# First products of the next stage between the last turns of two norms, projection weights by way of the raw buffer, and attention inputs turned a unit later

## The chip, the core and the metric

The kernel runs on one core of a Trainium2 chip. The metric is the device time of one execution in microseconds. The core has TensorE (PE in the profile; PEld is its weight load), VectorE (DVE), ScalarE (ACT), GpSimd (POOL) and SyncE (SP), each with a queue of its own, and 16 DMA engines. They meet only at semaphores.

## The reference

Two transformer layers on 1024 tokens of width 1024, all in float32. The parts that matter here, in the order in which the program comes to them:

```
h = rmsnorm(x, g_mix); z = h @ w_in                       # first layer
q_na, k_na = rmsnorm(...) per head; q = rmsnorm(q_mem); k, v = mem_n @ w_mem_kv
gates = sigmoid(gate_pre)                                  # 3 x 1024 columns of z
y = gates0 * (h_m @ w_proj_mlstm) + gates1 * (h_na @ w_proj_na) + gates2 * (h_mem @ w_proj_mem)
x = x + y @ w_out
u = rmsnorm(x, g_ffn) @ w_up                               # 4096 columns
x = x + square(relu(u)) @ w_down
h = rms_norm(x, attn_norm); proj = h @ w_in_2              # second layer: delta net, retention, experts
```

## The kernel before

The program is a chain of stages. Each stage is a block: every engine runs its own list for the stage, written out in the code, and all of them start the next block together. Within a block the order on an engine is fixed by the code, and an engine waits at a semaphore for what it needs. PSUM has eight banks of 128 x 512 numbers, `c.bank(i)`.

A float32 matrix product is made of three: each operand is split in an upper part (a rounded copy) and a lower part (the rest), and `PASSES` runs upper x upper, upper x lower and lower x upper. So a product over eight k tiles is 24 matmuls of 512 columns, and one over four k tiles is 12. Weights arrive in chunks of 1 MB: SP loads a chunk in the one raw buffer, `c.raw` (`load_chunks`, issued at L102); VectorE splits it in one of two places of `c.split_ring` (`split_chunk`), which takes a wait for the chunk two places back to be used up (`c.used`); TensorE waits for the split (`wait_split`). The next load waits for that split.

**Attention inputs** (`attention_inputs`). There are 18 units: 8 for q and k of the neighbourhood attention, 8 for its v and the memory's q, 2 for the memory's k and v. A unit is one block of 128 tokens; its product has two halves, r = 0 and r = 1, of 12 matmuls each with a weight chunk each. Units go in runs of four: the first halves of the run, then the second halves. After a unit's second half ScalarE copies and squares it, VectorE sums the squares, GpSimd takes the power -0.5, VectorE scales the rows (L1172), and TensorE turns them (L1071) in one of two banks, from which VectorE copies them (L1144) when it is at the unit two further on. TensorE keeps the finished units in the list `waiting`; a turn is put into its queue after a half product by rules on the length of that list. `NEXT_SPLIT` says before which unit VectorE splits the next weight chunk.

**Gated branches** (`gated_branches`). The gates are made first by `SevenProducts`: two blocks of columns as quarters in the ordinary way, and the other ten (W = 10) as seven half-size products each, for which VectorE and ScalarE make operands and sums. Results go out over tiles to DRAM (`gate_rows`). In the last of the ten blocks the steps turn over to the projections: SP loads the first two pieces of projection weights (v = 0, 1), VectorE splits them (`split_pw`), ScalarE takes the upper parts of the branches' outputs (`take_acts`), VectorE the lower ones (`lower_act`). Then TensorE does the 48 projections, which wait for `pw_split`, `acts_split` and the evictions, and VectorE multiplies each with the gates read back from DRAM.

**Norms at a stage's end** (`project_norm` and the end of `ffn`). The last product of a stage adds a residual, and each block of 128 tokens is normalised, turned by TensorE in two groups of four transposes (`TileNorm.turn`, L431, banks 0 to 3), copied as the upper part by ScalarE (L439) and as the lower part by VectorE (L138). The turn of a block follows the products by three blocks (`LAG`), so turns 5, 6 and 7 stand behind all products. Two of the three such norms are touched: the one before the feed-forward stage (`out1`) and the one at its end (`ff`).

**What comes behind them.** The feed-forward stage begins with `SevenProducts` again (eight quarters of 24 matmuls, then W = 14 blocks of seven products of 12), and the second layer with `delta_inputs`, 24 products of 24 matmuls for a convolution.

## Time and profile before

| | |
|---|---|
| three timed runs | 3031.94, 3036.04, 3036.41 us; median 3036.04 |
| the profiled execution's own time | 3034.09 us |
| its span, first to last instruction | 3032.3 us |
| granted TensorE clock, mean | 0.959 of full speed |
| TensorE busy | 2770.4 us, 91% |
| VectorE busy | 1456.2 us, 48% |
| ScalarE, GpSimd busy | 780.2 us, 345.8 us |

The stages of the change lie at these times of the span: attention inputs from 261 to 383 us, gates and projections from 515 to 850, the norm of `out1` up to 956, the feed-forward stage to 1635, `delta_inputs` to 1837. The experts of the second layer load their weights in the last 600 us, at around 400 GB/s.

In a timeline row stand the start, the time taken, the engine, the line of the kernel, the operation, what it writes and reads, its shape and how many instructions the row merges; in brackets the idle time of the engine before it and what ended that. "PEq" and "SPq" as a releaser or an engine are the queue of the engine. TensorE's matmuls are pipelined: one starts while the one before is in flight, so starts are compared, not ends.

### The profile page before, as it was taken

Reading aid. Unit: us, or ns where it says so; the run is one execution under the profiler, and the core shown is the slowest. Engines: PE = TensorE matmul, PEld = TensorE weight load, DVE = VectorE, ACT = ScalarE, POOL = GpSimd, SP = SyncE. Lnnn points to the kernel's source line nnn. Section 1 sums busy time; section 2 is a strip of 40 time slices with the busy share of each in tenths; the row PEclk is TensorE's granted clock in tenths of the full one; section 3 lists DMA queues with packets and bytes.
Section 4 is the critical chain, followed back from the end, with each engine's and each line's share of the span. In section 5 each row is a group of like instructions: output and inputs, shape, how many; then the busy total and the mean of one; then the engine's idle time right before and its main releaser. Section 6 shows DMA issues by size and latency. Waiting matters only on the chain. (4 is left out here: it accounts for less than half of the span.)

```text
span 3032.3 us, 43019 instructions
## 1 busy us (share of the span) xinstructions
PE 2770.4 (91%) x17136; PEld 2156.1 (71%) x17136; DVE 1456.2 (48%) x2428; ACT 780.2 (26%) x1729; POOL 345.8 (11%) x497
## 2 busy tenths in 40 slices
PE   7998988999999999999999998899999878888886
PEld 5876755887777888878887896777887745545443
DVE  6656487765756666543355643554434431111113
ACT  3244176433013555300003423330021201111111
POOL 1023300000001000000001003540020211111112
PEclk9998999999999999999999998999999979999998
DMA  4130121233632334432234220002102199999995
GB/s 149 43 91 18 56 93 34 93 112 118 198 122 97 102 111 139 170 108 94 84 97 99 46 39 2 2 2 70 42 18 109 66 385 417 415 414 406 404 399 210
DMA packets 162152, 430.08 MB, mean 142 GB/s; under 512 B 18585, under 2 KB 64793, under 8 KB 144545
## 3 DMA queue, kind: packets, MB, share of 16 engines
q1 hardware_dynamic: 146128, 392.04, 36.4%
q10 hardware_dynamic: 5312, 18.48, 1.7%
q0 software_dynamic: 10512, 16.80, 1.5%
q8 instruction: 137, 2.24, 0.3%
q14 instruction: 63, 0.51, 0.0%
HBM read 382.76 MB, written 65.08 MB: 148 GB/s over the span
## 5 line engine op out<-in xcount | busy, mean ns | idle before, releaser
L489 PE MATMUL banks<-split_weights,hT_upper 128*128 128x512 f32 x1536 | 482.9, 396 | 14.3 <-DVE hT_lower L138 8.6
L489 PEld LDWEIGHTS banks<-split_weights,hT_upper 128*128 128x128 f32 x1536 | 290.8, 191 | 76.9 <-issue 14.5
L489 PE MATMUL banks<-split_weights,uT_upper 128*128 128x512 f32 x1024 | 317.2, 391 | 2.7 <-DVE uT_lower L138 2.6
L489 PE MATMUL banks<-split_weights,hT_lower 128*128 128x512 f32 x768 | 303.0, 395 | 0.0
L3529 PE MATMUL banks<-expert_inner,ex_xT 128*64 128x256 f32 (+1 forms) x1248 | 217.6, 400 | 34.4 <-DVE ex_xT L3629 10.7
L498 PE MATMUL banks<-hT_upper,split_weights 128*128 128x512 f32 x736 | 234.0, 396 | 9.2 <-DVE split_weights L138 4.4
L3640 DVE COPY ex_y<-banks 128x512 f32<-128x512 f32 x36 | 24.9, 691 | 434.8 <-PE banks L3558 434.8
L489 PEld LDWEIGHTS banks<-split_weights,uT_upper 128*128 128x128 f32 x1024 | 192.6, 189 | 43.5 <-issue 3.5
L489 PE MATMUL banks<-split_weights,uT_lower 128*128 128x512 f32 x512 | 200.2, 391 | 0.0
L3529 PEld LDWEIGHTS banks<-expert_inner,ex_xT 128*64 128x64 f32 (+1 forms) x1248 | 139.6, 150 | 79.1 <-issue 47.6
L1901 PE MATMUL banks<-hT_upper,split_weights 128*128 128x512 f32 x576 | 189.1, 389 | 0.0
L138 DVE TENSOR_TENSOR split_weights<-raw_weights,split_weights 128x512 fp32r<-128x512 f32 (+1 forms) x128 | 177.7, 1388 | 5.0 <-ACT split_weights L1921 3.0
L489 PEld LDWEIGHTS banks<-split_weights,hT_lower 128*128 128x128 f32 x768 | 146.2, 190 | 31.3
L498 PEld LDWEIGHTS banks<-hT_upper,split_weights 128*128 128x128 f32 x736 | 140.4, 191 | 39.3 <-issue 5.4
L498 PE MATMUL banks<-hT_lower,split_weights 128*128 128x512 f32 x368 | 145.0, 394 | 0.0
L134 DVE CAST split_weights<-raw_weights 128x2048 fp32r<-128x2048 f32 x56 | 68.4, 1221 | 132.9 <-PE banks L489 42.8
L1901 PEld LDWEIGHTS banks<-hT_upper,split_weights 128*128 128x128 f32 x576 | 108.2, 188 | 22.3
L2207 DVE TENSOR_TENSOR x<-x,banks 128x512 f32<-128x512 f32 x64 | 43.9, 685 | 165.2 <-PE banks L489 165.2
L1901 PE MATMUL banks<-br_sums,split_weights 128*128 128x512 f32 x480 | 113.7, 389 | 0.0
L3558 PE MATMUL banks<-expert_inner,ex_hT 128*64 128x512 f32 (+1 forms) x312 | 106.3, 618 | 7.2 <-issue 6.4
L3529 PE MATMUL banks<-hT,ex_xT 128*64 128x256 f32 (+1 forms) x416 | 101.0, 399 | 12.5 <-DMA expert_inner<-in_w_up 5.9
L1901 PE MATMUL banks<-hT_lower,split_weights 128*128 128x512 f32 x288 | 112.1, 389 | 0.0
(554 smaller groups left out, 5074.0 us busy)
## 6 DMA issues: line engine op xcount, KB each, us to landing
expert_inner<-in_w_gate SPq DMA_DIRECT2D x39, 1024.0 KB, 13.1
expert_inner<-in_w_up SPq DMA_DIRECT2D x39, 1024.0 KB, 22.5
expert_inner<-in_w_down SPq DMA_DIRECT2D x38, 1024.0 KB, 24.5
raw_weights<-in_w_in SPq DMA_DIRECT2D x28, 1024.0 KB, 6.5
uT_whole<-u_rows ACTq DMA_DIRECT2D x32, 512.0 KB, 5.6
raw_weights<-in_w_down SPq DMA_DIRECT2D x16, 1024.0 KB, 5.1
raw_weights<-in_w_up SPq DMA_DIRECT2D x28, 512.0 KB, 4.1
hT<-in_w_gate SPq DMA_DIRECT2D x13, 1024.0 KB, 12.0
```

The source lines that it names most:

```text
L134: return engine.tensor_copy(dst.bitcast(F32R), src)
L138: return engine.tensor_tensor(dst.bitcast(F32R), whole, upper, ALU.subtract)
L489: last = pe.matmul(bank, acts[x][:, r * KT // 2 + k, m * P:(m + 1) * P].bitcast(F32R), w[y][:, k, :].bitcast(F32R), start=(r == 0 and k == ...
L498: last = pe.matmul(out, w[x][:, k, c0:c0 + P].bitcast(F32R), acts[y][:, k, t0:t0 + nt].bitcast(F32R), start=(k == 0 and x == y), stop=(k = ...
L1901: last = pe.matmul(self.bank(w, i), x_parts[x][:, k, :].bitcast(F32R), y_parts[y][:, k, :].bitcast(F32R), start=(k == 0 and x == y), stop= ...
L2207: nc.vector.tensor_tensor(x, x, c.bank(m), ALU.add).then_inc(added, 1)
L3529: last = nc.tensor.matmul(c.psum[cols, BANKS[q], i * D_EXPERT:(i + 1) * D_EXPERT], xT[:, q, k, cols], w[:, k, :], start=(k == 0), stop=(k ...
L3558: last = nc.tensor.matmul(c.psum[cols, 4 + b, :], hT[:, f, cols], experts.down[s][:, f, b * BANK:(b + 1) * BANK], start=(f == 0), stop=(f ...
L3640: nc.vector.tensor_copy(y[:, q, BANK:D], c.bank(5)).then_inc(y_dve, 1)
```

## The change

**Attention inputs.** The turn of a unit comes one half product later: while second halves run, a turn is put in only when more than four units wait (before: more than three), or when the run is the last one. The splits of the next chunks come before units 4, 8, 12 and 14 (before: 5, 8, 13 and 16). At the end both marks that the last two chunks are used are set together by ScalarE.

**Gated branches.** The first two pieces of projection weights are loaded in the raw buffer, when all operands of the last block are made, in place of another buffer when its third product is done. VectorE splits the first piece after the third step of the last block (before: after the fourth), and the lower parts of the first branch follow one step sooner as well. The load of the first chunk of `w_out` waits for both splits, since it overwrites the raw buffer.

**The two norms.** Behind turn 5, turn 6 and turn 7 stand eight matmuls each of the next stage's first product, in bank 4. They wait for that bank's last addition, the lower parts of the first four blocks of tokens, and the weights. The next stage leaves its first product out, and its banks are rotated by four, so that the rest follows on.

```diff
+def next_products(pe, c, hT, j, out):
+    w = c.parts(j)
+    for k in range(KT):
+        for x, y in PASSES:
+            yield pe.matmul(out, w[x][:, k, 0:P].bitcast(F32R), hT[y][:, k, 0:BANK].bitcast(F32R),
+                            start=(k == 0 and x == y), stop=(k == KT - 1 and x == 1))
+AHEAD_BANK = 4
...
-    NEXT_SPLIT = {5: C_NAV, 8: C_NAV + 1, 13: C_MEMKV, 16: C_MEMKV + 1}
+    NEXT_SPLIT = {4: C_NAV, 8: C_NAV + 1, 12: C_MEMKV, 14: C_MEMKV + 1}
...
-                            if len(waiting) > 3:
+                            if len(waiting) > RUN or run[-1] + 1 == n:
                                 turn(waiting.pop(0))
                             continue
-                        if i + 1 == n or (i == run[-1] and units[i + 1][0] != j):
+                        if i + 1 < n and i == run[-1] and units[i + 1][0] != j:
                             last.then_inc(c.used, 1)
...
-                if i + 1 == n or units[i + 1][0] != j:
+                if i + 1 == n:
+                    act.sem_inc(c.used, 2)
+                elif units[i + 1][0] != j:
                     act.sem_inc(c.used, 1)
...
+        raw = c.raw[:, :, :].rearrange("p k n -> p (k n)")
+        def pw_whole(v):
+            if v < 2:
+                return raw[:, v * D:(v + 1) * D].rearrange("p (a b n) -> p a b n", a=2, b=2)
+            return pw(h_plain[1], v)
...
                 else:
-                    sp.wait_ge(gates.product, 7 * (W - 1) + 3)
+                    sp.wait_ge(gates.made, 7 * W)
...
             def after_first(w):
                 if w == W - 1:
-                    for v in range(2):
-                        load_pw(v)
+                    sp.wait_ge(gates.product, 7 * w + 3)
                     gates.wait_stored(sp, 5)
...
-            gates.transfers(sp, after_first, None)
+            def after_block(w):
+                if w == W - 2:
+                    for v in range(2):
+                        load_pw(v)
+            gates.transfers(sp, after_first, after_block)
             gates.wait_stored(sp, 3 * N)
-            sp.wait_ge(gates.made, 7 * W)
+            sp.wait_ge(pw_split, 2)
             c.load_chunks(sp, C_OUT + 1)
...
-                if i == 3:
+                if i == 2:
                     split_pw(0)
-                if i in (4, 5):
-                    lower_act(0, 2 * (i - 4))
-                    lower_act(0, 2 * (i - 4) + 1)
+                if i in (3, 4):
+                    lower_act(0, 2 * (i - 3))
+                    lower_act(0, 2 * (i - 3) + 1)
...
+            soon = None if ahead is None else next_products(nc.tensor, c, acts, ahead, c.bank(AHEAD_BANK))
             for i in range(TT - LAG, TT):
                 norm.turn(pe, i)
                 route(i - 2)
+                if soon is not None:
+                    if i == TT - LAG:
+                        pe.wait_ge(added, TT + AHEAD_BANK + 1)
+                        pe.wait_ge(norm.copied, TT)
+                        c.wait_split(pe, ahead)
+                    for _ in itertools.islice(soon, KT):
+                        pass
...
     def bank(self, w, i):
-        return self.c.bank((7 * w + i) % 8)
+        return self.c.bank((7 * w + i + self.first_bank) % 8)
...
+            if i == 0 and self.first_done:
+                continue
+            last = split_channels(pe, self.quarter_bank(i), self.hT, (i % 2) * BANK, BANK, c.parts(j), (i // 2 % 2) * P)
+            last.then_inc(self.quarter, 2 if i == 1 and self.first_done else 1)
...
                             if f + n + h == 0:
-                                if m < 2:
-                                    pe.wait_ge(up.evicted, 7 * W - 1 + m)
+                                up.wait_bank(pe, m)
...
+            soon = next_products(nc.tensor, c, hT, C_IN2, c.bank(AHEAD_BANK))
             for i in range(TT - LAG, TT):
                 norm.turn(pe, i)
+                if i == TT - LAG:
+                    pe.wait_ge(added, LAST + AHEAD_BANK + 1)
+                    pe.wait_ge(norm.copied, TT)
+                    c.wait_split(pe, C_IN2)
+                for _ in itertools.islice(soon, KT):
+                    pass
...
                     if g >= NB:
                         pe.wait_ge(copied, g - NB + 1)
-                    split_channels(nc.tensor, c.bank(g % NB), hT, th * BANK, BANK, c.parts(C_IN2 + ch // 2), ch % 2 * P).then_inc(product, 1)
+                    if g:
+                        last = split_channels(nc.tensor, c.bank(AHEAD_BANK + g % NB), hT, th * BANK, BANK, c.parts(C_IN2 + ch // 2), ch % 2 * P)
+                        last.then_inc(product, 2 if g == 1 else 1)
```

TensorE's order at the end of the first norm, before: the last products of the stage (L489), the turns (L431, the last four as one row of 32 transposes), then the next stage's first product (L498).

```order
L489 MATMUL banks<-split_weights,hT_upper 128x512 x2
L489 MATMUL banks<-split_weights,hT_lower 128x512
L431 MATMUL banks<-c_ident,out_xn 128x128 x32
L1589 UNCONDITIONAL_BRANCH
L2105 UNCONDITIONAL_BRANCH
L498 MATMUL banks<-hT_upper,split_weights 128x512
L498 MATMUL banks<-hT_lower,split_weights 128x512
L498 MATMUL banks<-hT_upper,split_weights 128x512 x2
```

The same place now (L443 is the turn, L378 `next_products`): turns 4 and 5 in one row, eight matmuls, turn 6, and the beginning of the next eight.

```order
L443 MATMUL banks<-c_ident,out_xn 128x128 x16
L378 MATMUL banks<-hT_upper,split_weights 128x512
L378 MATMUL banks<-hT_lower,split_weights 128x512
L378 MATMUL banks<-hT_upper,split_weights 128x512 x2
L378 MATMUL banks<-hT_lower,split_weights 128x512
L378 MATMUL banks<-hT_upper,split_weights 128x512 x2
L378 MATMUL banks<-hT_lower,split_weights 128x512
L443 MATMUL banks<-c_ident,out_xn 128x128 x8
L378 MATMUL banks<-hT_upper,split_weights 128x512 x2
L378 MATMUL banks<-hT_lower,split_weights 128x512
```

The 24 matmuls of the next stage's first product moved in front of the two block ends, in three groups of eight behind the last three turns. The end of the `ff` norm reads likewise.

TensorE's order at the start of the last run of the attention inputs, before: the last product half of unit 15 (from hT), the turn of unit 12 (L1071), then the first half of unit 16 (from at_mem).

```order
L489 MATMUL banks<-split_weights,hT_upper 128x512 x2
L489 MATMUL banks<-split_weights,hT_lower 128x512
L1071 MATMUL banks<-c_ident,at_raw 128x128 x2
L489 MATMUL banks<-split_weights,at_mem_upper 128x512 x2
L489 MATMUL banks<-split_weights,at_mem_lower 128x512
```

The same place now (L1083 is the turn, L501 the products):

```order
L501 MATMUL banks<-split_weights,hT_upper 128x512 x2
L501 MATMUL banks<-split_weights,hT_lower 128x512
L501 MATMUL banks<-split_weights,at_mem_upper 128x512 x2
L501 MATMUL banks<-split_weights,at_mem_lower 128x512
L501 MATMUL banks<-split_weights,at_mem_upper 128x512 x2
L501 MATMUL banks<-split_weights,at_mem_lower 128x512
L501 MATMUL banks<-split_weights,at_mem_upper 128x512 x2
L501 MATMUL banks<-split_weights,at_mem_lower 128x512
L501 MATMUL banks<-split_weights,at_mem_upper 128x512 x2
L501 MATMUL banks<-split_weights,at_mem_lower 128x512
L1083 MATMUL banks<-c_ident,at_raw 128x128 x2
```

The turn of unit 12 moved behind unit 16's first half. In the same way each turn of the earlier runs stands one half product later.

VectorE's order in the last of the ten gate blocks, before: evictions of half-size products (L1970), the split of the first piece of projection weights (hT_upper, hT_lower from hT), the lower parts of the branches (branches_lower), the second split.

```order
L1970 TENSOR_TENSOR br_gate_pair<-hT_spare,banks 128x512
L1970 TENSOR_TENSOR hT<-hT_spare,banks 128x512
L134 CAST hT_upper<-hT 128x2x512
L138 TENSOR_TENSOR hT_lower<-hT,hT_upper 128x2x512
L1970 TENSOR_TENSOR br_gate_pair<-hT,banks 128x512
L1970 TENSOR_TENSOR hT_spare<-hT_spare,banks 128x512
L138 TENSOR_TENSOR branches_lower<-x,br_sums 128x1024 x2
L1970 TENSOR_TENSOR hT_spare<-hT,banks 128x512
L138 TENSOR_TENSOR branches_lower<-x,br_sums 128x1024 x2
L1970 TENSOR_TENSOR hT_spare<-hT_spare,banks 128x512
L134 CAST hT_upper<-hT 128x2x512
```

The same place now (L2020 is the eviction):

```order
L2020 TENSOR_TENSOR br_gate_pair<-hT_spare,banks 128x512
L134 CAST hT_upper<-raw_weights 128x2x512
L138 TENSOR_TENSOR hT_lower<-raw_weights,hT_upper 128x2x512
L2020 TENSOR_TENSOR hT<-hT_spare,banks 128x512
L138 TENSOR_TENSOR branches_lower<-x,br_sums 128x1024 x2
L2020 TENSOR_TENSOR br_gate_pair<-hT,banks 128x512
L2020 TENSOR_TENSOR hT_spare<-hT_spare,banks 128x512
L138 TENSOR_TENSOR branches_lower<-x,br_sums 128x1024 x2
L2020 TENSOR_TENSOR hT_spare<-hT,banks 128x512
L2020 TENSOR_TENSOR hT_spare<-hT_spare,banks 128x512
L134 CAST hT_upper<-raw_weights 128x2x512
```

The first split, now from the raw buffer, and the four lower parts moved up by one eviction each; the second split kept its place.

## Rows read from the trace of the kernel before

**Rows 1.** Section 1 of the page: busy us, share of the span, instructions.

```profile
PE 2770.4 (91%) x17136; PEld 2156.1 (71%) x17136; DVE 1456.2 (48%) x2428; ACT 780.2 (26%) x1729; POOL 345.8 (11%) x497
```

**Rows 2.** Busy us by stretch, down projection: PE, PEld, DVE, ACT, POOL, PEclk, DMA.

```profile
1268.00:1620.00 352.00, 349.42 (x1546) 289.12 (x1547) 155.78 (x160) 11.86 (x22) 5.31 (x11) 1.00 0.34 117
```

**Rows 3.** Timelines by engine, last gate block and first projection.

```profile
732.93 0.69 DVE L138 TENSOR_TENSOR split_weights<-raw_weights,split_weights 128x512 fp32r<-128x512 f32 x1
...
742.24 0.98 SPq L1463 DMA_DIRECT2D hT<-in_w_proj_mlstm  x2
...
743.21 3.90 ACT L1521 ACTIVATE br_sums<-x 128x1024 fp32r<-128x1024 f32 x4 [1.36 <-PE banks L1901]
...
746.99 0.69 DVE L134 CAST hT_upper<-hT 128x1024 fp32r<-128x1024 f32 x1 [3.09 <-DMA hT<-in_w_proj_mlstm]
...
752.92 2.35 DVE L138 TENSOR_TENSOR branches_lower<-x,br_sums 128x1024 fp32r<-128x1024 f32 x2
...
755.37 0.76 PE L1513 MATMUL banks<-br_sums,hT_upper 128*128 128x512 f32 x1 [4.04 <-issue]
...
761.35 0.40 PE L1513 MATMUL banks<-br_sums,hT_lower 128*128 128x512 f32 x1
```

**Rows 4.** Timelines by engine, attention inputs.

```profile
285.35 0.60 PE L1071 MATMUL banks<-c_ident,at_raw 128*128 128x128 f32 x4
...
296.56 0.76 DVE L1172 SCALAR_TENSOR_TENSOR at_raw<-at_raw,at_rstd 128x256 f32<-128x256 f32 x2 [2.70 <-POOL at_rstd L1134]
...
297.37 0.66 PE L1071 MATMUL banks<-c_ident,at_raw 128*128 128x128 f32 x4 [1.24 <-DVE at_raw L1172]
...
304.66 0.69 DVE L1162 TENSOR_REDUCE at_ss<-at_squares 128x16 f32<-128x512 f32 x1 [7.34 <-ACT at_squares L1125]
...
326.76 1.22 DVE L134 CAST split_weights<-raw_weights 128x2048 fp32r<-128x2048 f32 x1
...
333.42 0.38 ACT L1118 ACTIVATE at_raw<-banks 128x256 f32<-128x256 f32 x1 [20.27 <-PE banks L489]
...
369.35 1.22 DVE L134 CAST split_weights<-raw_weights 128x2048 fp32r<-128x2048 f32 x1
...
372.95 0.74 PE L489 MATMUL banks<-split_weights,at_mem_upper 128*128 128x512 f32 x2 [2.37 <-DVE split_weights L138]
...
382.12 0.58 PE L1071 MATMUL banks<-c_ident,at_raw 128*128 128x128 f32 x2 [2.39 <-DVE at_raw L1172]
```

**Rows 5.** Timelines by engine, first norm's end and the next stage.

```profile
947.58 1.16 PE L431 MATMUL banks<-c_ident,out_xn 128*128 128x128 f32 x8 [0.71 <-DVE hT_lower L138]
...
952.36 1.94 PE L431 MATMUL banks<-c_ident,out_xn 128*128 128x128 f32 x8 [1.23 <-DVE hT_lower L138]
...
954.97 0.69 DVE L138 TENSOR_TENSOR hT_lower<-banks,hT_upper 128x512 fp32r<-128x512 f32 x1 [0.16 <-ACT hT_upper L439]
...
955.98 0.77 PE L498 MATMUL banks<-hT_upper,split_weights 128*128 128x512 f32 x1 [1.68 <-PEq L1589]
...
963.21 0.60 ACT L1909 ACTIVATE ff_relu<-banks 128x512 f32<-128x512 f32 x1 [8.27 <-PE banks L498]
```

**Rows 6.** Busy time by stretch, at the ends of both norms.

```profile
950.00:955.00 5.00, 3.08 (x16) 2.35 (x16) 4.73 (x8) 2.38 (x5) 0.00 (x0) 0.73 0.00 0
...
1630.00:1635.00 5.00, 1.16 (x8) 0.84 (x8) 3.66 (x7) 1.35 (x3) 0.00 (x0) 1.00 0.00 0
```

**Rows 7.** Timelines by engine, second norm's end and the next stage.

```profile
1630.82 1.16 PE L431 MATMUL banks<-c_ident,ff_scratch 128*128 128x128 f32 x8 [1.23 <-DVE hT_lower L138]
...
1635.11 0.76 PE L498 MATMUL banks<-hT_upper,split_weights 128*128 128x512 f32 x1 [3.13 <-PEq L3764]
...
1642.48 0.60 ACT L2324 ACTIVATE di_raw<-banks 128x512 f32<-128x512 f32 x1 [9.86 <-PE banks L498]
```

**Rows 8.** Timelines by engine, start of the feed-forward stage's half-size products.

```profile
1001.09 0.39 PE L1901 MATMUL banks<-hT_upper,split_weights 128*128 128x512 f32 x1
...
1008.45 2.29 DVE L138 TENSOR_TENSOR branches_lower<-x,branches_lower 128x2048 fp32r<-128x2048 f32 x1 [1.98 <-ACT branches_lower L1927]
```

48 lines of the change are left out of this document (29 added, 19 removed).

## The prediction

> **What bounds the kernel now.** I read the page first: the busy shares, the 40 slices, the granted clock. TensorE is busy for 2770 of 3032 us [rows 1], and in the densest stage it starts 1546 matmuls in 352 us at the full clock [rows 2], so one 512-column matmul costs 0.227 us when nothing holds it (352.0/1546, the few transposes aside). Then I read TensorE's timeline in each stage that the diff touches and looked for two things: idle time with its releaser, and stretches in which the same matmul takes 0.427 us (14 starts from 755.37 to 761.35 [rows 3]), which is the low clock of 1.2 GHz against 2.4. Idle time of other engines I read only where one of them releases TensorE. A shift that TensorE gains in a stage is kept later on if each later stage starts on what the earlier one leaves; these stages are blocks in which all engines begin together.
>
> **The first part: attention inputs.** A unit is two half products of 12 matmuls, 12 x 0.227 = 2.73 us each, in runs of four units. Unit 3's second half ends at 285.35, where its first turn stands; the turn of unit 3 starts at 297.37, because its row is normalised only at 297.32 (296.56 + 0.76) [rows 4]. Behind that turn one more half product of the run follows before second halves start. With every turn one half product later, 285.35 + 4 x 2.73 + 3 x 0.4 = 297.5: the turn of unit 3 is no longer waited for, and nothing but it stands before the second halves. They start 2.7 us sooner.
>
> On VectorE the split of the next weight chunk stands between units 4 and 5. A split takes 3.5 us (the one at 369.35 releases TensorE for 372.95 [rows 4]), so 304.66 to 326.76, where the next split starts, is 22.1 us = 4 x 4.65 + 3.5 [rows 4], and the turns of units 5 to 7 wait for it. Moved ahead of unit 4 it falls into the 7.34 us of idle time that stand there [rows 4]; it waits for the end of the first halves of units 4 to 7, now 297.3, and ends at 301. Unit 4's sum starts at 304.66 - 2.7 = 302.0, the four units take 18.6, and the following split ends at 320.6 + 3.5 = 324.1. TensorE comes to the second halves of units 8 to 11 at 297.9 + 4 x 2.73 + 4 x 3.1 = 321.3 and waits for that split until 324.1. Before, ScalarE saw unit 8's product at 333.42 [rows 4], so these halves started at 330.5. Saved so far: 6.4. What is late next here is that split, for 2.8 us.
>
> The last stall is the split that starts at 369.35 [rows 4] and holds TensorE until 372.95 [rows 4]. It needs only that unit 15's product is done (then 324.1 + 8 second halves x 2.73 + 4 first halves with turns x 3.0 = 357.9), so put two units earlier it ends at 361.5, while TensorE comes for it at 357.9 + 2 x 3.0 = 363.9. Its 2.37 us idle row and the pipeline's 0.2 go. The part is worth **9.0 us**, and the last turn moves from 382.12 to 373.1. The cover: VectorE's copy of a turned unit i-2 sits in unit i's queue; it stands in the wait for GpSimd's power, which leaves 2.7 us idle after it [rows 4], and the turn comes 2.7 later. For units 2, 3, 6 and 7 I find the turned rows 2 to 3 us before that wait ends. If the cover is gone, each of the four costs up to the 2.7 us by which its turn moved, 10.8 in all, and the part gives nothing (0). A gain beyond 11.8 is excluded, since only the 2.8 us wait for the split is left.
>
> **The second part: projection weights.** SP's queue issues four loads from 742.24 on (two in the row, two behind it), after a wait for the last block's third product; VectorE waits 3.09 us for them in the middle of the last block [rows 3]. The two splits and four lower parts follow it, and the fourth lower part ends at 752.92 + 2.35 = 755.27; TensorE has ended the block's last product at 751.2 and starts at 755.37 with 4.04 idle [rows 3]. By way of the raw buffer, free once the last block's operands are made (732.93 + 0.69 = 733.6 [rows 3]), the loads go out 8 us sooner. They pass one 256 KB store of results, which then leaves 2 us later; its tile is written again only at 752. The split runs at 741.1 to 743.1, directly behind the third eviction. ScalarE makes the upper parts at 743.21 to 747.1 as before [rows 3]; lower parts stand at 744.4 to 746.7 and 748.0 to 750.3, before 751.2. The 4.1 us stall goes, and with it the slow matmuls behind it, 14 x (0.427 - 0.227) = 2.8. VectorE's first multiply then comes at 758.6 and has caught up by the fourth product (762.1). Sum **6.9 us**. Bounds: 4.1 if the clock falls all the same, 0 if the loads land after 746.9; the value is at the upper end, because nothing in these rows leaves TensorE idle.
>
> **The third part: products between the last turns, twice.** In the first norm the last three turns wait for lower parts, 2.39 us apart: turn 5 at 947.58, turn 6 at 949.97, turn 7 at 952.36; VectorE ends at 955.66 (954.97 + 0.69), and the next stage starts at 955.98 with the first of its 24-matmul products; ScalarE gets it at 963.21 [rows 5]. That is 7.06 us of TensorE, 24 x 0.227 = 5.45 and 1.6 of low clock. After: turn 5, 8 matmuls (1.82 us), turn 6 at 950.3 instead of 949.97, 8 matmuls, turn 7 at 952.95 instead of 952.36, 8 matmuls to 955.6. The turn itself takes 1.94 us in a stretch granted 0.73 [rows 5, 6] and about 1.0 at the full clock, so VectorE's end moves from 955.66 to about 955.5 and TensorE's is 955.8: the stage starts 0.15 later. Gain 7.06 - 0.15 = **6.9 us**. In the second norm the last turn takes 1.16 at 1630.82 already at the full clock [rows 6, 7]; there it only moves by 0.6, and so does the stage's start (1635.11). The first product took 1635.11 to 1642.3 [rows 7], 7.2: gain **6.6 us**. All waits that the new products carry (the bank's last addition, the first four tiles' lower parts, the weight split) are over by 948.1. Bounds for 24 matmuls in this place: 0.227 each as in rows 2 and 0.427 as in rows 3, so 5.45 to 10.2 us; I take the nearer, since the idle time between turns goes.
>
> The chip's rule on this, in the Trainium skill, TensorE: Matmul & The Clock Gate, "HAM oscillation — how this bites in real kernels", is that an idle gap makes the clock gate close and the matmuls after it pay at half rate; its Part 4 adds that transposes do not count as busy. The fall to 0.73 during turns alone agrees, and by that rule the inserted products hold the clock up, as the sum has it. Against it speaks that the second norm's turns, also alone, were granted 1.00. If only the gaps counted, the three later places would give 4.1 + 5.3 + 4.8 instead of 6.9 + 6.9 + 6.6, and the sum would be 23.2, 3012.
>
> Does the next stage take up the shift? Its eighth product ends and the half-size ones start at 1001.09 [rows 8]; now 6.9 sooner at 994.2. The operands come from VectorE. Even if none of its work moved, its last sum part (1008.45 + 2.29 = 1010.7 [rows 8]) meets a need at 994.2 + 6 x 2.73 = 1010.6. ScalarE no longer waits for products in between, so I expect it 5 us sooner. Bank numbers rotate by four and cost nothing; each bank waits for its own last eviction, which frees 0.15 us at the handover at most. The experts' loads are first issued after the last norm, so they shift too.
>
> **Sum.** 9.0 + 6.9 + 6.9 + 6.6 = 29.4. The profiled execution took 3034.09 (span 3032.3 and 1.8 around it): 3004.7. The three timed runs have a median of 3036.04, 1.9 above it: 3006.6. I forecast 3006.
>
> **Rivals.**
> 1. The low clock comes anyway in the norms' ends. Then 24 matmuls cost 4.8 more in each, and each next stage still starts slow (1.6): 29.4 - 2 x 6.4 = 16.6, 3019. For it: the 0.73 row. Against: no idle time is left there, and the second norm's turns ran at 1.00 even with idle time between them [rows 6]. Chance 0.08.
> 2. The later turns hold up VectorE, so that the first part gives 0 to 3: 3006 + 6 to 9, 3012 to 3015. For it: the order of its queue. Against: 2.7 us of power wait cover each. Chance 0.08.
> 3. A load, a split or ScalarE's bunched evictions take one of the later stalls' places; one of the 7 us terms is lost: 3013. Chance 0.10.
> 4. The gain is not the program's: the early work only moves, because blocks end at other engines, or the experts' loads are the end of everything. 3030 to 3036. Against: VectorE and TensorE end the norms within 0.3 us of each other, and the first products are gone from the next stage. Chance 0.03.
> 5. Slower: the granted clock is rationed over the execution. Its mean is 0.96; denser work would lower it elsewhere. It decides against the change from 29.4/2770 = 1.1% of clock, from 0.959 to under 0.949; at 1.5% it costs 41.6, so 3036 + 12 = 3048. Against: 352 us at 99% busy at 1.00 [rows 2]. Chance 0.02.
>
> The forecast's own chance is 0.69, 3001 to 3010 (the first part up to 2.8 better, the runs 2 us apart). The range, 2999 to 3018, takes in rivals 2 and 3 and most of 1. A measurement of this kernel can tell 0.2%, 6 us, from no change. Faster 0.95, same 0.03, slower 0.02.
>
> **What would show it.** Right: no idle row at the turns of units 2 to 7 but one of about 2.8 us at the second halves of unit 8; the matmul after 751 follows at once and at 0.227; 24 matmuls among the last three turns at 0.227; the stage behind begins with 0.2 to 1.7 us of idle and at full clock; 48-matmul pairs reach ScalarE 5.5 us after it. Wrong: VectorE idle for turned rows inside a unit, a multiply that waits for gate loads after 758, a turn 7 later by more than 1 us, or idle before the half-size products at 994.

## The result and the profile after

The changed kernel takes 3003.95 us (median of four runs, 2999.52 to 3009.75) against 3033.99 us in four runs of the kernel before on the same chip (3031.84 to 3036.41). The measured ratio is 0.9907 (the two medians alone would make 0.9901), 95% interval 0.9889 to 0.9924, so it is faster. The forecast was 3006 in 2999 to 3018. The profiled execution is the fastest of the four, 2999.52 us with a span of 2997.8. Section 1 of its page, to set beside [rows 1] (TensorE does the same 17136 matmuls in 18 us less of busy time; the mean granted clock of the two profiles is 0.967 against 0.959):

```profile
PE 2752.0 (92%) x17136; PEld 2143.2 (71%) x17136; DVE 1456.0 (49%) x2428; ACT 778.9 (26%) x1729; POOL 345.7 (12%) x497
```

**Attention inputs**, timelines by engine (start, us, engine, line, operation, [idle before <- what ended it]):

```profile
284.40 0.60 PE L1083 MATMUL banks<-c_ident,at_raw 128*128 128x128 f32 x4
...
294.24 1.23 DVE L134 CAST split_weights<-raw_weights 128x2048 fp32r<-128x2048 f32 x1 [0.58 <-PE banks L501]
...
308.04 0.60 PE L1083 MATMUL banks<-c_ident,at_raw 128*128 128x128 f32 x4
...
317.12 1.22 DVE L134 CAST split_weights<-raw_weights 128x2048 fp32r<-128x2048 f32 x1
...
317.61 0.60 PE L1083 MATMUL banks<-c_ident,at_raw 128*128 128x128 f32 x4
320.73 0.98 PE L501 MATMUL banks<-split_weights,hT_upper 128*128 128x512 f32 x2 [2.52 <-DVE split_weights L138]
321.51 0.63 PE L501 MATMUL banks<-split_weights,hT_lower 128*128 128x512 f32 x1
...
325.38 0.39 ACT L1132 ACTIVATE at_raw<-banks 128x256 f32<-128x256 f32 x1 [18.41 <-PE banks L501]
```

The turns of units 2 to 7 have no idle row (six of them between 284.40 and 317.61; in [rows 4] the one at 297.37 waited 1.24). The split that was named as late next is late by 2.52 us (forecast 2.8). What was not forecast stands behind it: the pair at 320.73 takes 0.78 to the next start and single matmuls 0.427, so unit 8's product reaches ScalarE 4.65 us after TensorE's start. In the kernel before it took 3.06 (TensorE's start at 330.36, ScalarE at 333.42 [rows 4]). Nine intervals at or near 0.427 for 0.227 are about 1.7 us lost. The last split no longer holds TensorE (2.37 us in [rows 4]).

**Last gate block and first projection**, the queue of SyncE, VectorE and TensorE, to set beside [rows 3]:

```profile
722.62 0.90 SPq L1485 DMA_DIRECT2D raw_weights<-in_w_proj_mlstm  x2
...
740.94 0.69 DVE L134 CAST hT_upper<-raw_weights 128x1024 fp32r<-128x1024 f32 x1
741.66 1.22 DVE L138 TENSOR_TENSOR hT_lower<-raw_weights,hT_upper 128x1024 fp32r<-128x1024 f32 x1
...
737.42 2.88 PE L1951 MATMUL banks<-br_sums,split_weights 128*128 128x512 f32 x12
740.14 0.39 PE L1539 MATMUL banks<-br_sums,hT_upper 128*128 128x512 f32 x1
740.36 0.39 PE L1539 MATMUL banks<-branches_lower,hT_upper 128*128 128x512 f32 x1
```

The loads go out 17.5 us ahead of the first projection and nobody waits for them. The first projection starts 2.72 us behind the start of the gates' last twelve matmuls, 12 x 0.227, so directly behind them and at the full clock. The idle 4.04 us and the slow matmuls of before are gone.

**The two norms**, TensorE from the third last turn of the first norm on, the FFN's first matmul and first half-size one [rows 8], the delta inputs' first; then the stretches that answer to [rows 6]:

```profile
929.70 1.16 PE L443 MATMUL banks<-c_ident,out_xn 128*128 128x128 f32 x8 [0.71 <-DVE hT_lower L138]
930.62 0.47 PE L378 MATMUL banks<-hT_upper,split_weights 128*128 128x512 f32 x1
...
932.55 1.03 PE L443 MATMUL banks<-c_ident,out_xn 128*128 128x128 f32 x8
...
935.27 1.03 PE L443 MATMUL banks<-c_ident,out_xn 128*128 128x128 f32 x8
...
938.43 0.47 PE L510 MATMUL banks<-hT_upper,split_weights 128*128 128x512 f32 x1 [0.30 <-PEq L1615]
...
976.63 0.39 PE L1951 MATMUL banks<-hT_upper,split_weights 128*128 128x512 f32 x1
...
1609.84 0.47 PE L510 MATMUL banks<-hT_upper,split_weights 128*128 128x512 f32 x1 [1.43 <-PEq L3823]
```

```profile
929.00:934.00 5.00, 4.30 (x27) 3.74 (x28) 5.00 (x7) 3.92 (x8) 1.62 (x2) 1.00 0.26 105
934.00:939.00 5.00, 4.70 (x26) 3.67 (x25) 3.42 (x6) 1.36 (x3) 0.10 (x1) 1.00 0.00 0
...
1605.00:1610.00 5.00, 3.57 (x21) 2.74 (x20) 2.81 (x7) 1.09 (x2) 0.00 (x0) 1.00 0.00 0
1610.00:1615.00 5.00, 5.00 (x23) 4.13 (x23) 3.47 (x2) 0.00 (x0) 0.00 (x0) 1.00 0.46 124
```

The last turn starts 5.57 us behind the third last (4.78 in [rows 5]) and takes 1.03 instead of 1.94. The next stage starts with 0.30 idle, at the full clock (0.47 for its first matmul against 0.77 in [rows 5]), and comes to the half-size products 38.20 us later instead of 45.11 [rows 5, 8]. The delta inputs start with 1.43 idle instead of 3.13 [rows 7], also at the full clock.

### The profile page after: what moved, and what is told of

It reads as the page before. It is cut to its first block and busy times, and to the rows that moved or that the text cites. A ratio compares the mean times of both kernels' runs of the same rounds, so it can differ in the third digit from the quotient of the medians.

```text
span 2997.8 us, 43021 instructions
## 1 busy us (share of the span) xinstructions
PE 2752.0 (92%) x17136; PEld 2143.2 (71%) x17136; DVE 1456.0 (49%) x2428; ACT 778.9 (26%) x1729; POOL 345.7 (12%) x497
## 5 line engine op out<-in xcount | busy, mean ns | idle before, releaser
L501 PE MATMUL banks<-split_weights,hT_upper 128*128 128x512 f32 x1536 | 483.1, 396 | 16.4 <-DVE hT_lower L138 8.6
L501 PEld LDWEIGHTS banks<-split_weights,hT_upper 128*128 128x128 f32 x1536 | 290.9, 191 | 79.4 <-issue 15.0
L501 PE MATMUL banks<-split_weights,uT_upper 128*128 128x512 f32 x1024 | 315.8, 389 | 3.0 <-DVE uT_lower L138 3.0
L501 PE MATMUL banks<-split_weights,hT_lower 128*128 128x512 f32 x768 | 303.4, 395 | 0.0
L510 PE MATMUL banks<-hT_upper,split_weights 128*128 128x512 f32 x704 | 222.3, 394 | 6.1 <-DVE split_weights L138 4.4
L501 PEld LDWEIGHTS banks<-split_weights,uT_upper 128*128 128x128 f32 x1024 | 191.9, 188 | 42.9 <-issue 3.4
L501 PE MATMUL banks<-split_weights,uT_lower 128*128 128x512 f32 x512 | 199.2, 389 | 0.0
L1951 PE MATMUL banks<-hT_upper,split_weights 128*128 128x512 f32 x576 | 189.0, 389 | 0.0
L501 PEld LDWEIGHTS banks<-split_weights,hT_lower 128*128 128x128 f32 x768 | 146.4, 191 | 31.2
L510 PEld LDWEIGHTS banks<-hT_upper,split_weights 128*128 128x128 f32 x704 | 133.4, 189 | 35.0 <-DVE split_weights L138 4.5
L510 PE MATMUL banks<-hT_lower,split_weights 128*128 128x512 f32 x352 | 138.1, 392 | 0.0
L1951 PEld LDWEIGHTS banks<-hT_upper,split_weights 128*128 128x128 f32 x576 | 108.1, 188 | 22.4
L1951 PE MATMUL banks<-hT_lower,split_weights 128*128 128x512 f32 x288 | 112.0, 389 | 0.0
```

What stands on the lines that cost most here:

```text
L501: last = pe.matmul(bank, acts[x][:, r * KT // 2 + k, m * P:(m + 1) * P].bitcast(F32R), w[y][:, k, :].bitcast(F32R), start=(r == 0 and k == ...
L510: last = pe.matmul(out, w[x][:, k, c0:c0 + P].bitcast(F32R), acts[y][:, k, t0:t0 + nt].bitcast(F32R), start=(k == 0 and x == y), stop=(k = ...
L1951: last = pe.matmul(self.bank(w, i), x_parts[x][:, k, :].bitcast(F32R), y_parts[y][:, k, :].bitcast(F32R), start=(k == 0 and x == y), stop= ...
```

## How the gain is counted

The profiled spans differ by 34.5 us, more than the touched stages give. TensorE comes to the first touched stage at 256.94 instead of 261.10 ([4.36 idle] in both), ahead of any change. In all 14 profiles of this study that point lies between 254.01 and 261.10, by no pattern of the kernels. So I count each part between two marks of TensorE, starts of matmuls that both kernels have. "Without" and "with" are the profiles of kernels that leave that part as it was and that have it as in the changed kernel; the gain is the difference of the means:

| from, to | without the part | with it | gain |
|---|---|---|---|
| attention inputs' first matmul to the attention's first | 122.4 to 122.8 (4 profiles) | 115.3 to 115.7 (4) | 7.0 |
| gates' first matmul to out1's first | 337.9 to 338.4 (5) | 330.8 to 332.2 (8) | 6.6 |
| out1's first to the FFN's first half-size product | 146.7 to 147.6 (4) | 140.9 to 141.8 (8) | 6.1 |
| delta inputs' first to the 6.03 us wait for dr_g | 207.9 to 209.0 (4) | 200.9 to 201.0 (8) | 7.5, less a start 0.6 later: 6.9 |

Kernels that change a part in another way are left out of its row: after_filler, after_held, held_again, held_split and turns_only in the first, held_split (329.4) in the second, products_behind in the third and fourth, norm_fillers in both of these. In the first row norm_fillers (124.3) is left out too, since its 2.37 us wait drew the clock down. All are told of below.

Two rows mix stretches of different clock. In the third, a_only (146.7) began the FFN at the full clock without any ahead product (its clock had fallen one turn earlier, at 938.8, and was back), and three of the eight (141.6 to 141.8) had a longer slow stretch at the start of out1. Where both are alike, 147.6 in three profiles stands against 140.9 to 141.1 in five, 6.6 us. For the start in the fourth row I compare the time from the down products' first matmul to the delta inputs' first, in profiles whose clock fell at the down products: 342.6, 342.6, 343.0 and 343.0 without, 343.4 in four with it, so 0.4 to 0.8 later.

Together 26.6 us. The two timed comparisons of this kernel give 30.0 (3033.99 less 3003.95) and 26.1 us (3033.12 less 3007.04) by their medians, 28.2 and 27.6 by their ratios.

## Experiments

### Each part alone

`a_only` holds the changed turn rule, NEXT_SPLIT and marks of the attention inputs, `b_only` the way of the projection weights, `c_only` and `d_only` the ahead products of one norm; the rest of each is the kernel before.

> Only the attention inputs are changed (turns one half product later, splits ahead of units 4, 8, 12, 14); the rest is the kernel before. Theory 1, the size read from the profiled pair: the part is worth 6.6 us, since TensorE waits 2.5 us for the split ahead of unit 8's second half and then runs that product at the low clock, 1.8 us of loss that the prediction left out; ratio 0.9978. Theory 2, the prediction's term: 9.0 us, ratio 0.9970, and the fall of the clock behind that wait was chance: it will be missing in this profile, where unit 8's product then takes 2.9 us from TensorE's start to ScalarE instead of 4.65. Theory 3, the shift isn't handed on by the attention: 0 us, ratio 1.000.

> Only the path of the projection weights is changed (loads into the raw buffer behind the last block's operands); the rest is the kernel before. Theory 1: 6.9 us (4.1 of stall and 2.8 of slow matmuls), ratio 0.9977, and in the profile the first projection product stands directly behind the gates' last half-size product at 0.227 us for each matmul. Theory 2, the low clock comes anyway: 4.1 us. Theory 3, the loads fit only because the attention inputs ended sooner: 0 to 3 us, ratio 0.999 or more, with an idle row for the loads in VectorE's timeline.

> Only the first norm's change (the FFN's first product between its last three turns, with the rotation of the FFN's banks); the rest is the kernel before. Theory 1: 6.5 us (24 matmuls at 0.227 and the 1.6 us of low clock of the next stage's start, less a start 0.15 to 0.35 later), ratio 0.9979. Theory 2, only the gaps between turns count and the next stage starts slow all the same: 5 us. Theory 3, the FFN's stage is set by its operands from VectorE and takes the shift back: 0 to 2 us.

> Only the second norm's change (the recurrent stage's first product between its last three turns); the rest is the kernel before. Theory 1: 6.2 us (read from the profiled pair; the prediction had 6.6), ratio 0.9980. Theory 2, only the gaps count: 4.8 us. If the four parts stand side by side without helping each other, the gains of the four runs sum to that of the changed kernel, 27 to 30 us.

| kernel | median us (11 runs) | ratio | interval |
|---|---|---|---|
| before (33 runs) | 3033.59 | | |
| a_only | 3023.76 | 0.9973 | 0.9964 to 0.9982 |
| b_only | 3025.43 | 0.9974 | 0.9965 to 0.9983 |
| c_only | 3029.51 | 0.9986 | 0.9977 to 0.9995 |
| d_only | 3028.13 | 0.9977 | 0.9968 to 0.9986 |

The ratios give 8.2, 7.9, 4.2 and 7.0 us, each give or take 2.7; their sum, 27.3, is that of the changed kernel. So no help or hindrance between the parts shows, within the some 5 us that four such errors make together, and b_only shows that its loads do not need the earlier attention inputs (first projection at 749.91, no idle row). The times alone don't tell 6.6 from 9.0 us in the first part: both lie within the interval. The profile of a_only does. It has the same wait and nearly the same slow stretch as the changed kernel (7 matmuls at 0.427 there, 8 here, and a partly slow one at each end):

```profile
320.58 0.91 PE L489 MATMUL banks<-split_weights,hT_upper 128*128 128x512 f32 x2 [2.51 <-DVE split_weights L138]
321.29 0.63 PE L489 MATMUL banks<-split_weights,hT_lower 128*128 128x512 f32 x1
321.72 1.05 PE L489 MATMUL banks<-split_weights,hT_upper 128*128 128x512 f32 x2
```

Theory 2, that the fall behind this wait was chance, is not borne out; two more profiles below have the same wait and the same fall. c_only came out lower in time than its marks (6.6), within its interval.

### What the wait ahead of unit 8's second half costs

`after_filler` puts 11 matmuls into that wait; nothing reads their result (operands cut short here):

```
+if first == 2 * RUN and r:
+    pe.wait_ge(taken, NB + 1)
+    for x in range(11):
+        nc.tensor.matmul(c.bank(0), hT[x % 2][:, x % 4, 0:P]..., c.wide_parts(j)[0][:, x % 4, :]..., start=True, stop=True)
 c.wait_split(pe, j + r)
```

> The changed kernel with 11 matmuls (2.5 us at 0.227) whose result nothing reads, in the 2.52 us in which TensorE waits for the split ahead of unit 8's second half. Theory 1, the fall of the clock behind that place (9 matmuls at 0.427, 1.7 us) comes from TensorE standing idle there: no slow matmul follows, unit 8's product takes 2.9 us to ScalarE instead of 4.65, and the part of the profile from the stage's start to the attention's shrinks from 115.7 to 114.0 us, 1.7 us faster than the changed kernel. Theory 2, the clock falls by a count of its own whatever stands there: the slow matmuls stay, and the time is that of the changed kernel.

Its timelines of TensorE (two rows) and ScalarE:

```profile
319.81 0.39 PE L1097 MATMUL banks<-split_weights,hT_upper 128*128 128x512 f32 x1
320.18 0.73 PE L501 MATMUL banks<-split_weights,hT_upper 128*128 128x512 f32 x2
...
323.23 0.38 ACT L1137 ACTIVATE at_raw<-banks 128x256 f32<-128x256 f32 x1 [16.80 <-PE banks L501]
```

The same wait for the same split, filled: the matmuls behind it run at the full clock and unit 8's product arrives 3.05 us after its start instead of 4.65. The stage takes 113.6 us against 115.7; 1.6 of the difference is here, the rest a shorter slow stretch at the stage's start. Theory 1 holds: idle time of TensorE draws the clock down, and that cost 1.7 us. The total, 3007.81 us (ratio 0.9913, 0.9898 to 0.9927), can't show so small a sum. By the rule in the Trainium skill, TensorE: Matmul & The Clock Gate, "HAM oscillation — how this bites in real kernels", an idle gap closes the clock gate for the matmuls behind it. This pair of traces agrees in kind. The page asks for a longer gap than the 2.52 us here, and on that the measurement decides.

### The splits against the later turns

`turns_only` is the changed kernel with the four splits in their old places.

```
-    NEXT_SPLIT = {4: C_NAV, 8: C_NAV + 1, 12: C_MEMKV, 14: C_MEMKV + 1}
+    NEXT_SPLIT = {5: C_NAV, 8: C_NAV + 1, 13: C_MEMKV, 16: C_MEMKV + 1}
```

> The changed kernel with the old places of the four splits (ahead of units 5, 8, 13, 16), so that of the attention inputs only the later turns are new. By the prediction's sum the later turns alone give 2.7 us and the moved splits 3.7 + 2.6: so 6.3 us slower than the changed kernel by it, with an idle row of 2.4 us again ahead of units 16 and 17's second halves. Rival: the turn rule is what matters and the splits hide anyway: within 2 us of the changed kernel.

3016.73 us, ratio 0.9941 (0.9929 to 0.9954): 10 to 13 us slower than the changed kernel by the medians. The stage takes 125.85 us (256.02 to 381.87), against 115.5 with the moved splits and 122.5 in the kernel before. Later turns alone make it 3.3 us slower, where I had given them a gain of 2.7. TensorE at its two longest waits for a split, and VectorE at the stage's end:

```profile
322.93 1.22 PE L501 MATMUL banks<-split_weights,hT_upper 128*128 128x512 f32 x2 [2.81 <-DVE split_weights L138]
...
368.79 1.22 PE L501 MATMUL banks<-split_weights,at_mem_upper 128*128 128x512 f32 x2 [4.31 <-DVE split_weights L138]
...
361.53 0.42 DVE L1158 TENSOR_TENSOR qmT<-banks,c_g_heads 128x256 f32<-128x256 f32 x1 [1.95 <-PE banks L1083]
...
364.51 0.42 DVE L1158 TENSOR_TENSOR qmT<-banks,c_g_heads 128x256 f32<-128x256 f32 x1 [1.90 <-PE banks L1083]
...
365.18 1.22 DVE L134 CAST split_weights<-raw_weights 128x2048 fp32r<-128x2048 f32 x1
```

VectorE's copies of units 12 and 13 stand ahead of the split in its queue and now wait for turns that come one product later; the split follows them, and TensorE waits 4.31 us for it with 12 slow matmuls behind (2.37 us and none in [rows 4]). From the stage's first matmul TensorE is at unit 8's second half after 66.9 us (69.3 in the kernel before), so the later turns did gain 2.4 us up to there. The slow matmuls behind the 2.81 us wait take back 1.2, the longer last wait 1.9 and the slow matmuls behind it 2.2: more than half of what was lost is the clock's. The late split is rival 2 of the prediction, at a place where no wait for GpSimd covers it. With the split ahead of unit 14 it stands before those copies and the cost is gone.

### The position of the ahead products

`products_behind` makes all 24 behind the last turn in both norms.

> The changed kernel with all 24 ahead matmuls behind the last turn in both norms, instead of 8 behind each of the last three. Theory 1, what the interleaving gives is cover (TensorE's waits between turns) and the clock: in the first norm they end 3.4 us later at the full clock and up to 8 us later at the low one; in the second, where the block ends 3.1 us behind the last turn anyway, 2 us later. Together 5.4 to 8 us slower than the changed kernel. Theory 2, only the two stages' first product leaves the start of the next stage, wherever it stands: the same time as the changed kernel.

3016.00 us, ratio 0.9940 (0.9927 to 0.9952): 9 to 12 us slower than the changed kernel by the medians, somewhat more than expected. Its first norm, and the last turn of its second:

```profile
938.08 1.83 PE L443 MATMUL banks<-c_ident,out_xn 128*128 128x128 f32 x8 [1.23 <-DVE hT_lower L138]
939.56 0.78 PE L378 MATMUL banks<-hT_upper,split_weights 128*128 128x512 f32 x1
940.13 0.63 PE L378 MATMUL banks<-hT_lower,split_weights 128*128 128x512 f32 x1
...
946.54 0.47 PE L510 MATMUL banks<-hT_upper,split_weights 128*128 128x512 f32 x1 [0.30 <-PEq L1615]
...
1614.44 1.94 PE L443 MATMUL banks<-c_ident,ff_scratch 128*128 128x128 f32 x8 [1.23 <-DVE hT_lower L138]
```

```profile
937.00:942.00 5.00, 3.92 (x15) 3.48 (x16) 4.11 (x7) 1.68 (x3) 0.00 (x0) 0.66 0.00 0
...
1612.00:1617.00 5.00, 3.72 (x18) 3.27 (x19) 4.78 (x7) 2.45 (x5) 0.00 (x0) 0.71 0.02 3
```

From out1's first matmul to the FFN's first it takes 107.3 us against 102.9, so 4.5 us are lost there: what no longer lies between the turns, and the turn itself and the first matmuls behind it at the low clock. Theory 2 is refuted. The clock fell at the second norm's last turn too (0.71), where it was 1.00 in [rows 6], and from the down products' first matmul to the delta inputs' first it takes 347.7 us against 343.4: 4.3 us lost, where 2 were expected.

`norm_fillers` asks the opposite: the kernel before, with 24 matmuls among the last three turns of both norms whose result nothing reads; the next stages still make their first product.

```
-    x_out=(x1_dram, x1_stored))
+    x_out=(x1_dram, x1_stored), ahead=C_FFN)
+    soon = next_products(nc.tensor, c, hT, C_IN2, c.bank(AHEAD_BANK))
```

> The kernel before with 24 matmuls whose result nothing reads among the last three turns of both norms, 8 behind each; the next stages still make their first product themselves. Theory 1, the prediction's: they cost what they cover (0.15 to 0.35 us in the first norm, 0.6 to 0.8 in the second) and keep the clock up, so that each next stage starts at the full clock and its first product loses 1.5 us less: 2.1 us faster than before in all. Theory 2, the clock at the start of a stage falls with the 1.4 to 3.1 us between the stages whatever stood ahead: 1.0 us slower.

3032.82 us, ratio 0.9996 (0.9987 to 1.0005): 2 us aren't resolved, and neither theory is refuted by the time. In its profile the FFN starts with 0.30 idle and its half-size products come 43.63 us later (45.11 before), and the delta inputs take 206.39 us against 207.9 to 209.0: 1.5 us or more in each stage by the clock alone. For the second norm that is firm: all four profiles with nothing between its turns began the delta inputs slowly, all ten with matmuls there did not. For the first it is less so: three of four began the FFN slowly, but a_only, without any fillers, at the full clock (second fence), with 43.61 us to its half-size products. And the fillers' cost eats most of it: from out1's first matmul to the FFN's half-size products norm_fillers takes 147.5 us, as the kernel before. TensorE at the FFN's start in norm_fillers and in a_only:

```profile
952.34 0.47 PE L510 MATMUL banks<-hT_upper,split_weights 128*128 128x512 f32 x1 [0.30 <-PEq L1601]
```

```profile
944.54 0.47 PE L498 MATMUL banks<-hT_upper,split_weights 128*128 128x512 f32 x1 [1.80 <-PEq L1591]
```

### One kernel twice, and how often the clock falls

> The changed kernel once more. In all traces so far the wait for the last hidden parts ahead of the down products (2.6 to 3.4 us) was followed by 7 or 8 matmuls at 0.427 us, 1.4 to 1.65 us lost, but not in two of the seven with that wait at 2.97 or 2.98. If such falls are chance, one of the places differs here between two profiles of one kernel; then a single profiled pair carries 1 to 2 us of luck at each wait of this length. If the kernel sets them, the slow stretches stand at the same places and cost the same: 9 or so matmuls behind the 2.52 us wait ahead of unit 8's second half, none ahead of the down products. Time 3004, ratio 0.9907.

3007.04 us, ratio 0.9909 (0.9892 to 0.9926). Its TensorE ahead of the down products, second fence, beside the first profile of the same kernel, first fence:

```profile
1268.09 0.70 PE L501 MATMUL banks<-split_weights,uT_upper 128*128 128x512 f32 x2 [2.98 <-DVE uT_lower L138]
1268.62 0.39 PE L501 MATMUL banks<-split_weights,uT_lower 128*128 128x512 f32 x1
1268.86 0.62 PE L501 MATMUL banks<-split_weights,uT_upper 128*128 128x512 f32 x2
```

```profile
1268.86 0.70 PE L501 MATMUL banks<-split_weights,uT_upper 128*128 128x512 f32 x2 [3.08 <-DVE uT_lower L138]
1269.40 0.39 PE L501 MATMUL banks<-split_weights,uT_lower 128*128 128x512 f32 x1
1269.62 0.88 PE L501 MATMUL banks<-split_weights,uT_upper 128*128 128x512 f32 x2
1270.30 0.63 PE L501 MATMUL banks<-split_weights,uT_lower 128*128 128x512 f32 x1
```

After nearly the same wait the clock falls in one execution (7 matmuls at 0.427, 1.4 us) and not in the other. In the 14 profiles it fell here in ten. Behind the 2.52 us wait ahead of unit 8 it fell in all four profiles that have it, with 6 to 8 matmuls at 0.427, so that loss belongs to the kernel. The first profile of the changed kernel was lucky at the down products by 1.6 us (341.8 us to the delta inputs, against 343.4). That, the head's 4.2 us, 1.2 us in the attention (131.0 us to the gates, against 132.2) and 2.2 us behind the last mark make up what the one pair's 34.5 us have beside the four parts, 25.4 us in this pair.

### Two steps further

`after_held` removes the wait that the change left: the split goes ahead of unit 7's sum, and the turn of unit 7, which that delays, is held back until unit 8's second half is out.

```
-    NEXT_SPLIT = {4: C_NAV, 8: C_NAV + 1, 12: C_MEMKV, 14: C_MEMKV + 1}
+    NEXT_SPLIT = {4: C_NAV, 7: C_NAV + 1, 12: C_MEMKV, 14: C_MEMKV + 1}
-    if len(waiting) > RUN or run[-1] + 1 == n:
+    if len(waiting) > RUN or run[-1] + 1 == n or i == 2 * RUN:
-    if waiting:
+    if waiting and i + 1 != 3 * RUN:
```

> The changed kernel with the split of C_NAV+1 one unit earlier (ahead of unit 7's sum) and the turn of unit 7 held back until unit 8's second half is out. Theory 1: the split ends at 316.0 instead of 320.7, TensorE goes from unit 11's first half (317.6) straight to unit 8's second half, and both the 2.5 us wait and the 1.7 us of slow matmuls go; less one turn that only moves: 3.9 to 4.2 us faster than the changed kernel, 2.8 of it the wait that the prediction named as late next; stage 111.6 to 111.9 us. Rival: VectorE, which then does unit 7's sum 3.5 us later and three units behind it, becomes late for the turns of units 8 to 11; then 0 to 2 us.

> The kernel with the split ahead of unit 7's sum and the turn of unit 7 held back, once more, beside the changed kernel on one chip: its profile had the attention inputs in 111.6 us against 115.7. Expected 4.2 us faster than the changed kernel (3000), ratio to the kernel before 0.9893. If the gain is given back later: the same time as the changed kernel.

The wait is gone; in its place the held turn waits a quarter microsecond:

```profile
321.34 0.65 PE L1083 MATMUL banks<-c_ident,at_raw 128*128 128x128 f32 x4 [0.25 <-DVE at_raw L1186]
```

The stage takes 111.6 and 111.5 us in two profiles (115.4 and 115.7 in the changed kernel), 4.0 us less. Timed, it has 3002.32 (ratio 0.9894, 0.9880 to 0.9909) and 3005.07 us (0.9896, 0.9881 to 0.9911): better in both comparisons by about what was expected, but not apart from 0.9907 and 0.9909 by their intervals.

`held_split` adds the split of the gates' first weight chunk, moved from the gates' start into VectorE's idle time ahead of the attention's last copy.

```
+    if i == n + 2:
+        c.split_chunk(dve, C_BRANCH)      # in the attention, ahead of take(n - 1)
-    c.split_chunk(dve, C_BRANCH)          # at the start of the gates
```

> The kernel with unit 7's turn held back, and besides the split of the gates' first weight chunk moved from the start of the gates into the end of the attention, where VectorE is idle for 2.57 us ahead of its last copy. The split takes 3.5 us, so the last copy is 0.9 late, and TensorE starts the gates at once instead of 4.36 us behind its last attention matmul: 2.6 us sooner by VectorE's rows, and up to 1 us more if the slow stretch at the gates' start gets shorter with the wait. Expected 2.6 to 3.6 us faster than the kernel without it. Rival: the next split waits for its load at 508.97 in any case and the gates' second chunk becomes the stall; then 0.

TensorE at the start of the gates, in held_again and in held_split:

```profile
500.14 0.80 PE L510 MATMUL banks<-hT_upper,split_weights 128*128 128x512 f32 x1 [4.36 <-DVE split_weights L138]
500.73 0.63 PE L510 MATMUL banks<-hT_lower,split_weights 128*128 128x512 f32 x1
```

```profile
496.70 0.47 PE L510 MATMUL banks<-hT_upper,split_weights 128*128 128x512 f32 x1 [1.48 <-PEq L1224]
497.01 0.40 PE L510 MATMUL banks<-hT_lower,split_weights 128*128 128x512 f32 x1
```

The idle time is 1.48 instead of 4.36, and no slow matmuls follow: from the gates' start to out1's it takes 329.4 us against 330.8 to 332.2 in the eight profiles of the table's second row. So the clock gives 1.4 to 2.8 us, where I had allowed it 1. The wait gives less than the 2.9 us by which the idle time shrank, since the attention ends later for the split: from the attention's first matmul to the gates' it takes 129.6 us. That is 1.5 less than in held_again (131.1), and 2.1 to 2.8 less than in the profiles whose clock was low as long at the attention's start as here (131.7 to 132.4); 2.6 were expected.

It is the fastest kernel here by its median: 2996.61 us (2993.95 to 3002.39), ratio 0.9884 (0.9869 to 0.9899). The interval excludes the changed kernel's values, 0.9907 and 0.9909, but overlaps their intervals, and it doesn't tell this kernel from the held one (0.9894 and 0.9896).

## Why the prediction was right, point by point

**The forecast and its range.** 3006 in 2999 to 3018; measured 3003.95 and 3007.04. The sum of the four terms was 29.4, the marks give 26.6. Most of what is missing is in the first term. The value was hit closer than the sum deserved: the forecast took 3036.04 for the kernel before, which the four runs put at 3033.99, and the two errors, 2.8 us of gain too much and 2.0 us of start too much, nearly cancel (3033.99 less 26.6 is 3007.4).

**Attention inputs, 9.0; measured 7.0.** The order of the timeline came as worked out: no waits at the turns, TensorE at unit 8's second half at 320.73 (forecast 324.1 in the old trace's time, which is 319.9 behind a head 4.16 us shorter), the last split out of the way. So 5.5 us were saved up to there, where the sum had 6.4. The larger miss is behind it. The step that was mis-sized is the sentence that the split "is late next here, for 2.8 us": it was priced as the wait alone. The wait also draws the clock down, 1.2 to 1.7 us more in four profiles, though the same prediction counted just that, 2.8 us of slow matmuls, for the stall that it removed in the second part. And its division between the edits was wrong: the later turns alone lose 3.3 us (forecast a gain of 2.7), and the moved splits are worth 10.3 (forecast 6.3). The forecast looked for VectorE's copies waiting for turned rows in units 2, 3, 6 and 7, not in 12 and 13.

**Projection weights, 6.9; measured 6.6 over all profiles and 7.1 in b_only.** In the first pair it is 6.0, since the changed kernel's profile had the longer slow stretch at the gates' start (10 matmuls at 0.427 against 6), which is no part of the change. The wait of 4.04 and the slow matmuls both went, the late store cost nothing, and VectorE's later multiplies cost TensorE nothing that the marks show.

**First norm, 6.9; measured 6.6 where the slow stretches around it are alike, 6.1 over all.** 5.45 us of cover (24 matmuls done in what was idle time) and 1.5 of clock, less a start 0.3 to 0.4 later (forecast 0.15). The 1.5 us is there only when the FFN would have begun slowly, in three of four profiles. norm_fillers shows it alone, products_behind what is lost when the cover is missing.

**Second norm, 6.6; measured 6.9.** The start came 0.4 to 0.8 later (forecast 0.6), and the first product was worth 7.0 to 8.1, as the slow stretch that it replaces varies from run to run.

**The rivals.** Rival 1 (low clock at the norms' ends) did not come: 1.00 in all four stretches. The other reckoning, that the gaps alone would count, had 4.1, 5.3 and 4.8 for the three later places; the marks give 6.6, 6.1 to 6.6 and 6.9, so it is refuted for the first and the third and unlikely for the second. Rival 2 did not come in the changed kernel, but turns_only shows that it was only the moved splits that kept it away. Rival 3 and rival 4 did not come: the shifts of TensorE are in the marks of every later stage. Rival 5, a rationed clock, did not come: the mean granted clock is 0.960 to 0.967 in the nine runs of the changed kernel, 0.959 in the forecast's profile of the kernel before and 0.957 to 0.963 in the fifteen runs beside after_again.

## What to carry to other kernels

Price a stall of TensorE as its wait and the slow matmuls behind it, both where one goes and where one is left; here 2.5 to 4.4 us of waiting cost 1.1 to 2.8 us more wherever the clock fell, and it fell at most of these waits. When a consumer in an in-order queue is moved back, look for the producers that stand behind its results in the other queue: the later turns paid only with the splits moved ahead.

Work of the next stage fits into the last waits of a stage only if it stands between them; behind them it costs its full time and runs at the clock that the waits have left.

## What the runs showed of the hardware

- Whether the clock falls after a wait of 2.4 to 3.4 us is chance in part: ahead of the down products ten times in 14, for the same kernel once and once not (2.98 and 3.08 us of wait; the held kernel likewise, 3.17 and 3.06). Behind the wait of 2.37 us for the last split in [rows 4] it did not fall in four profiles and did in norm_fillers (5 matmuls at 0.427).
- The same row of turns without other work kept the full clock in the second norm of the kernel before and of b_only (1.16 us for the last turn). It lost it at the last turn in a_only, c_only and products_behind (1.91 to 1.94 us). One window of one profile is no evidence that a stretch keeps its clock; the prediction used [rows 6] so.
- The time to the first touched stage varies by 7 us between profiles of kernels that don't differ up to there, 0.2% of the whole and as much as one whole part of this change gives. The time from the last mark, the wait for dr_g, to the end of the span varies more, from 1187.0 to 1197.4 us, also where no kernel of this study differs. So a single pair of spans says little about one part. Why they vary stays open; no run here tried it.
